# Two attention loops of a fused decoder kernel: row maxima ahead of the weight residues, and the second block's key and value panel between its two query panels

## Time and profile before

| | |
|---|---|
| median of three runs | 876.21 us (875.73 to 877.57) |
| profiled execution | 874.22 us, of which the span of the core is 872.4 us |
| TensorE (PE) busy | 815.5 us, 93% of the span |
| VectorE (DVE) busy | 549.2 us, 63% |
| ScalarE (ACT) busy | 420.5 us, 48% |
| GpSimd (POOL) busy | 115.0 us, 13% |
| mean granted TensorE clock | 0.978 of full speed |
| HBM | 119.48 MB read, 138 GB/s over the span |

### The profile page before, as it was taken

How to read it: one execution, slowest core, us unless ns; L and a number is a source line. 1 busy time by engine, 2 the same in 40 slices (tenths; PEclk the granted TensorE clock), 3 DMA queues, 4 the chain that set the end, 5 groups by cost and what they waited for, 6 DMA issues and landing times.

```text
span 872.4 us, 13760 instructions
## 1 busy us (share of the span) xinstructions
PE 815.5 (93%) x5402; PEld 721.7 (83%) x5402; DVE 549.2 (63%) x930; ACT 420.5 (48%) x820; POOL 115.0 (13%) x114
## 2 busy tenths in 40 slices
PE   5989898998969899999999999998999999999996
PEld 4768786876868677899988988888997788999995
DVE  5898666746895745444834757776674746555555
ACT  5434726744554634446536435554444435444443
POOL 1335004521441302000000000011000000000000
PEclk9999988999989999999999999998999999999999
DMA  9646222023543133463432544333454546655541
GB/s 311 198 154 205 85 72 74 1 72 120 181 131 107 54 109 108 153 200 131 145 121 73 162 129 145 97 98 119 160 181 145 193 145 217 195 192 193 184 155 48
DMA packets 93504, 121.42 MB, mean 139 GB/s; under 512 B 8760, under 2 KB 69616, under 8 KB 93440
## 3 DMA queue, kind: packets, MB, share of 16 engines
q1 hardware_dynamic: 92432, 117.80, 42.0%
q0 software_dynamic: 432, 1.57, 0.5%
q10 hardware_dynamic: 576, 1.17, 0.4%
HBM read 119.48 MB, written 1.05 MB: 138 GB/s over the span
## 4 chain that ended last, share of the span: by engine, by line
PE 75%; DVE 13%; ACT 4%; issue 3%; POOL 1%; POOLq 0%; DVEq 0%; ACTq 0%
PE bank L407 20%; PE bank L409 19%; PE bank L408 19%; DVE w_lo L1407 3%; PE bank L584 2%; PE bank L537 1%; PE bank L551 1%; ACT w_hi L1026 1%; PE bank L531 1%; ACT tmp L1124 1%; PE bank L892 1%; PE bank L414 1%; PE bank L413 1%; DVE small L1496 1%; DVE xres L1578 1%
## 5 line engine op out<-in xcount | busy, mean ns | idle before, releaser
L1407 DVE TENSOR_TENSOR w_lo<-raw,w_hi 128x1024 fp32r<-128x1024 f32 x216 | 267.0, 1242 | 154.7 <-ACT w_hi L1026 152.5
L1026 ACT CAST w_hi<-raw 128x1024 fp32r<-128x1024 f32 (+1 forms) x217 | 226.1, 1045 | 203.4 <-PE bank L409 181.6
L407 PE MATMUL bank<-h_hi,w_hi 128*128 128x256 f32 (+1 forms) x800 | 231.3, 289 | 2.6 <-DVE ar L1484 1.8
L408 PE MATMUL bank<-h_lo,w_hi 128*128 128x256 f32 (+1 forms) x800 | 228.1, 285 | 0.0
L409 PE MATMUL bank<-h_hi,w_lo 128*128 128x256 f32 (+1 forms) x800 | 227.4, 284 | 0.0
L407 PEld LDWEIGHTS bank<-h_hi,w_hi 128*128 128x128 f32 x800 | 152.5, 191 | 7.9 <-issue 3.4
L408 PEld LDWEIGHTS bank<-h_lo,w_hi 128*128 128x128 f32 x800 | 152.7, 191 | 0.3
L409 PEld LDWEIGHTS bank<-h_hi,w_lo 128*128 128x128 f32 x800 | 152.9, 191 | 0.0
L407 PE MATMUL bank<-w_hi,h_hi 128*128 128x512 f32 (+1 forms) x288 | 114.7, 398 | 11.5 <-DVE w_lo L1407 6.3
L409 PE MATMUL bank<-w_hi,h_lo 128*128 128x512 f32 (+1 forms) x288 | 112.6, 391 | 0.0
L408 PE MATMUL bank<-w_lo,h_hi 128*128 128x512 f32 (+1 forms) x288 | 112.1, 389 | 0.0
(11 more groups left out here) (309 smaller groups left out, 1245.1 us busy)
## 6 DMA issues: line engine op xcount, KB each, us to landing
raw<-in_w_in SPq DMA_DIRECT2D x24, 1024.0 KB, 5.2
raw<-in_a_w_in SPq DMA_DIRECT2D x14, 1024.0 KB, 5.2
raw<-in_w_ffn_gate SPq DMA_DIRECT2D x11, 1024.0 KB, 5.4
raw<-in_w_ffn_up SPq DMA_DIRECT2D x11, 1024.0 KB, 5.3
raw<-in_w_ffn_down SPq DMA_DIRECT2D x11, 1024.0 KB, 4.9
raw<-in_b_w_in SPq DMA_DIRECT2D x9, 1024.0 KB, 5.3
raw<-in_w_gate SPq DMA_DIRECT2D x8, 1024.0 KB, 5.3
raw<-in_a_w_out SPq DMA_DIRECT2D x4, 1024.0 KB, 5.1
```

The lines of the kernel that those rows point to most:

```text
L407: mm(o, lh, rh, start=start, stop=False)
L408: mm(o, lh, rl, start=False, stop=False)
L1026: nc.scalar.copy(split(w_hi, s), rawsub(s)[0]).then_inc(S["hi_ready"], 1)
L1407: V.tensor_tensor(split(w_lo, s), rawsub(s)[0], split(w_hi, s).bitcast(F), ALU.subtract).then_inc(S["lo_ready"], 1)
```

## The change

1. In both loops VectorE takes maxima and factors first; z gates and the rest follow, and the residues of the weights come last in a step, those that ScalarE has rounded a step earlier. ScalarE's roundings also move to the end of its step. In block 0 the residues of the four sub-chunks that the loop itself splits are spread to steps 10, 13 and 16 (`z_done`).
2. Block 0's compressed softmax is cut into four pieces that VectorE does in steps 0 to 3 of the loop; the transposes go to step 5 and bank 5, and quad 0's compressed values follow `pv(5)` instead of going ahead of `pv(0)`.
3. From job 4 (block 0) or 6 (block 1) on, scores rotate over banks 0 to 3, once the z tiles have left banks 0 and 1. `scores(j)` then waits for the exponentials of job j - 4.
4. In block 1 the key and value panel comes between the query panels (the order of the chunks in memory traffic follows), heads 0 to 7 are transposed ahead of the last quarter of the second query panel, keys after z tile 0, and heads 8 to 15 after z tile 1.
5. The transposes of the meta tokens go behind `scores(0)`, and the rest of their work on VectorE to the step after the last job's maxima.

```diff
-    tm("b_q", b, 512)
     add("b_kv", ...)
+    tm("b_q2", b, 512)
...
         def z_done(phase, j):
-            return 5 + min(j, 3) if phase == 0 else 3 + min(j, 5)
+            return 5 + min(max(j - 7, 0) // 3, 3) if phase == 0 else 3 + min(max(j, 0), 5)
+
+        def score_bank(phase, j):
+            return ps[2 + j % 2 if j < J4[phase] else (j - J4[phase]) % 4]     # J4 = (4, 6)
...
# TensorE, scores(j)
-                    if j >= 2:
-                        pe.wait_ge(S["p_exp"], j0 + j - 1)
+                    r = j - J4[phase]
+                    if r in (0, 1):
+                        pe.wait_ge(S["z_free"], 8 * phase + 7 + r)
+                    elif j >= 2:
+                        pe.wait_ge(S["p_exp"], j0 + j - 1 if r < 0 else j0 + j - 3)
...
# TensorE, block 1 ahead of its loop
             first_panel(1, first["b_q"], (0, 1))
-            tm_panel(first["b_q"] + 4, hx(h_hi), hx(h_lo), (2, 3))
+            tm_panel(first["b_kv"], hx(h_hi), hx(h_lo), (4, 5), width=256, rows=4)
+            tm_panel(first["b_q2"], hx(h_hi), hx(h_lo), (2, 3), last_q=3)
+            for tt in range(2):
+                pe.wait_ge(S["rp_out"], 9 + tt)
+                head_transposes(tt, 1, q_half(tt, 0))
+            tm_panel(first["b_q2"], hx(h_hi), hx(h_lo), (2, 3), first_q=3)
...
# VectorE, the loop
                 for j in range(n + LAG + 3):
-                    split_lo_to(z0 + z_done(phase, j) + RING)
-                    if phase and 1 <= j <= 5:
-                        z_gate(phase, 2 + j)
-                    if phase and j == 2:
-                        meta_tokens()
                     if j < n:
                         maxima(j)
                     if 1 <= j <= n:
                         factors(j - 1)
+                    if phase and 1 <= j <= 5:
+                        z_gate(phase, 2 + j)
+                    if phase == 0 and 1 <= j <= 2:
+                        z_gate(phase, 5 + j)
+                    if phase == 0 and j < 4:
+                        (compressed_sums, compressed_shift, compressed_factors, compressed_weights)[j]()
+                    if phase and j == 1:
+                        meta_tokens()
+                    if phase and j == n:
+                        meta_halves()
+                    if phase == 0 and j == 5:
+                        dve.wait_ge(S["cm_pt"], 1)
+                        V.tensor_copy(pcT, ps[5][:, :]).then_inc(S["cm_ptsb"], 1)
...
+                    split_lo_to(z0 + z_done(phase, j - 1) + RING)
...
# VectorE, block 1 ahead of its loop
+            base = first["b_q"] + 4
             for i in range(2):
+                split_lo_to(base + RING - 1 + i)
+                rope_item(10 + i, 11 + i, i, 8, 4, i, q8(i, 0), 8 + i)
+            for i in range(2):
+                split_lo_to(base + 2 + RING - 1 + i)
+                rope_item(12 + i, 13 + i, 4 + i, 2, 5, i, kd[2][:, i, 0:2], 10 + i)
...
+            for i in range(2):
+                q_lo(i, 12, 8 + i, i, 0)
+            split_lo_to(base + 5 + RING)
...
+            for i in range(2):
+                split_lo_to(base + RING - 1 + i)          # base = first["b_z"]
+                rope_item(14 + i, 15 + i, 2 + i, 8, 4, i, q8(i, 1), 12 + i)
+            z_gate(1, 0)
+            for i in range(2):
+                key_lo(2 + i, 10 + i, 0, i, 2)
+            split_lo_to(base + 1 + RING)
+            z_gate(1, 1)
+            for i in range(2):
+                q_lo(4 + i, 12, 12 + i, i, 1)
```

More of the change, by code:

```diff
@@ L427, in tm_half, with tm_panel @@
                 return last
-            def tm_panel(name_s, xh_, xl_, banks, width=512, rows=2):
-                for q in range(KT // rows):
+            def tm_panel(name_s, xh_, xl_, banks, width=512, rows=2, first_q=0, last_q=None):
+                for q in range(first_q, KT // rows if last_q is None else last_q):
                     s = name_s + q
@@ L506, in q_tiles, with q_half @@
                 return [[qr[:, tt, P * k:P * k + P] for k in range(4 * half, 4 * half + 4)] for half in range(2)]
+            def q_half(tt, half):
+                return [[qr[:, tt, P * k:P * k + P] for k in range(4 * half, 4 * half + 4)]]
             def k_tiles(i, groups):
@@ L563, in compressed_values @@
                         half = f // 4
-                        mm(ps[6 + quad % 2][:, T * (f % 2):T * (f % 2) + T], vblk[half][:, P * (f % 4):P * (f % 4) + P], pw[:, :, half, :],
-                           start=f % 2 == 0, stop=True, skip_group_check=f % 2 == 1)
+                        last = mm(ps[6 + quad % 2][:, T * (f % 2):T * (f % 2) + T], vblk[half][:, P * (f % 4):P * (f % 4) + P], pw[:, :, half, :],
+                           start=quad > 0 and f % 2 == 0, stop=True, skip_group_check=quad == 0 or f % 2 == 1)
+                    return last
                 def pv(j):
@@ L573, in pv @@
                         pe.wait_ge(S["og_ready"], 4 * phase + quad - 1)
-                    if phase == 0 and j % JQ[phase] == 0:
+                    if phase == 0 and quad and j % JQ[phase] == 0:
                         compressed_values(quad)
```

154 lines of the change are left out of this document (82 added, 72 removed).

## The result

| | before | after |
|---|---|---|
| median | 876.88 us (875.73 to 877.57, 4 runs) | 863.78 us (862.09 to 864.82, 4 runs) |
| ratio | | 0.985, interval 0.983 to 0.987 |
| profiled execution, span | 874.22, 872.4 us | 864.82, 863.0 us |
| mean clock of its TensorE | 0.978 | 0.982 |

The change gains 13.1 us by these medians; forecast were 7.3. The same kernel measured again (run after_again) gave 863.78 us against 875.14 of before (ratio 0.9861, 0.9842 to 0.9881), so 11 to 13 us is the gain. The direction was right and the size too small.

A forecast was written before the change was run, and what follows sets the result against it. TensorE was taken as nearly full (815.5 of 872.4 us), with VectorE or a ring of waits bounding around block 1's start. -3.7 - 4.4 + 0.8 = -7.3 us gave 866.9, plus 2.0 for the median 868.9 us; range 866 to 872.

The forecast's parts named there:

- term 1: Start of block 0's loop: job 8 starts 4.7 us earlier, 1.0 of it only put off, so 3.7 us gained.
- term 2: Block 1 ahead of its loop: the new panel order lets the loop begin 1.1 us earlier.
- term 3: Block 1's loop: exponentials released first bring the last pv 4.4 us earlier, with term 2 in it.
- the allowance for the clock: Loss of 0.8 us allowed for half clock behind TensorE's new waits in both blocks; ends 0 and 3.5.
- Cost 0, at most 1 us: Block 0's loop: residues spread to steps 10, 13 and 16 fit, leaving VectorE at 78%.
- the ring: Block 1's loop: from step 6 on VectorE's cycle of waits was to be the bound, taking back some gain.
- 4.7 us a step before: Block 1's loop: each of the old first steps was a ring of 4.7 us, against 4 us after.
- The replay: The new instruction lists of the changed stretches worked through with the old trace's durations, all at 2.4 GHz.
- Rival 1: No POOL and VectorE contention, clock stays up, block 1's meta work hides: 11.2 us less, 865.0 us; chance 0.14.

The follow-up runs named there:

- u_zdone: The changed kernel with the residues of block 0's loop's last four weight sub-chunks back in steps 1 to 3 instead of 10, 13 and 16: 866.4 us.
- zsteps: The changed kernel with block 0's three weight residues on VectorE in steps 9, 12 and 15 instead of 11, 14 and 17: 863.9 us.
- u_banks: The changed kernel with only the banks put back, scores in banks 2 and 3 alone: 867.0 us.
- meta_late: The changed kernel with the four meta token operations (meta_halves) behind block 1's loop instead of ahead of the last copy: 863.5 us.
- u_loop1: The changed kernel with only the order inside block 1's loop put back (weight rounding, residue and z gate ahead of the maxima): 866.9 us.
- fill: The changed kernel with unneeded matmuls in three TensorE waits (block 0's key transposes, block 1's z tile 0 and last transposes): 863.6 us.
- before_fill: The kernel before with unneeded matmuls in four TensorE waits, at block 0's loop start and ahead of block 1's loop: 872.9 us.
- best: The changed kernel with meta_halves behind the loop, residues of z tiles 0 and 1 ahead of the first query residues, and fills in four places: 856.75 us.
- best2: The kernel of best with block 0's loop residues in steps 9, 12 and 15: 858.4 us.

## Why the prediction fell short

**What bounds, and where.** Right: the gain is in the three stretches named, and behind them 0.35 us. Right as well that TensorE's waits and its clock are all there is to gain. Of the 4.3 us between the forecast 7.3 and the 11.6 of the stretches, 0.7 are in term 1, 0.2 in term 2, 2.6 in term 3, and 0.8 are the allowance for the clock. By the trace of after_again they are -0.1, -0.3, 2.7 and 0.8. Term 3 is the miss in both.

**Term 1, 3.7 forecast, 4.4 measured (3.6 in after_again).** The start gained more: job 8 is 20.83 us behind scores(0), forecast 22.6 and before 27.32. TensorE's wait at the compressed transposes was 1.48 and not 2.3 us, with 0.54 for POOL ahead of it, and scores(1) came 5.03 us behind scores(0) for 5.81, since z tile 6 ran at half for a shorter time; in after_again that step takes 5.90, and job 8 comes at 21.67. So 0.8 us of the difference is luck with the clock. "Cost 0, at most 1 us" for the spread residues failed: 1.2 us, two times 0.6, as u_zdone and zsteps show. VectorE takes them in steps 11, 14 and 17, each of which has a copy too; the two late places follow 11 and 17, which have the residues of a result besides. Behind them the next maxima and factors are late, and POOL with them (the wait of 0.37 us at 156.50; scores(14) to scores(15) take 2.52 us for 1.93). A busy share of 78% did not say that there was room in each step. The change of banks was to gain nothing in this full part; in the new order it gains 0.8 us (u_banks), at these same two places. In the old order, of which the forecast spoke, it wasn't tested.

**Term 2, 1.1 forecast, 1.3 measured (0.8 in after_again).** VectorE was idle for 2.11 us ahead of the residues of heads 0 to 7 (2.3 forecast), and TensorE waited 2.88 us at z tile 0 (2.7) and 2.61 at the last transposes (2.9); only the first of the two waits there was 0.17 for 2.1.

**Term 3, 3.3 more forecast, 5.9 measured: the step that failed.** It has the sentence "From step 6 on VectorE's ring is the bound". From scores(0) the forecast has scores(5) at 21.2 us, (8) at 27.6, (11) at 36.6 and the last product at 45.8; measured were 20.56, 26.79, 34.33 and 43.22 (after_again: 20.48, 26.72, 34.26 and 43.15). Most of the miss is between jobs 8 and 11: 9.0 us forecast, 7.54 measured. From job 6 to job 8 the distances are 1.98 and 1.93 us, TensorE's own work without a wait, and from job 8 to job 11 it waits only 0.72 us for POOL and 0.38 for VectorE's copy. The steps ahead of job 5 add 0.6 us to the miss, jobs 5 to 8 0.2, and the end 0.3. VectorE and POOL do hold each other up, with the durations forecast (a residue of 1.97, a multiplication of 1.94 us). The wait of 0.72 us stands behind that multiplication; it is what the contention costs here, and 1.0 was taken for it. So the ring was there, but nearly hidden behind TensorE's work. meta_halves were right: 1.1 us at the last copy (meta_late). "4.7 us a step before" was an average over unlike steps: 5.17 (half clock), 3.55, 3.95, 4.66, 6.57. u_loop1 shows that the old order costs nothing up to scores(4) and 4.2 us in all behind it. Before, scores(8) come 35.10 us behind scores(0): the forecast had gained 7.5 us there and gave 4.2 back by the end of the loop, measured are 8.3 and 2.4. Scores(8) in the trace of before:

```profile
294.97 0.50 PE L531 MATMUL bank<-msk,crr 128*128 128x512 f32 x1
```

**The clock, +0.8 forecast.** The replay ran at 2.4 GHz, so its terms already held what the old half-clock stretches cost, without naming it; the 0.8 us were for new ones behind the new waits. Those cost nothing: none behind the compressed transposes, one at z tile 0 that VectorE hides (fill), and in block 1's loop the clock is 1.00 for 0.93. In after_again one in front of that loop costs 0.5 us. Rival 1 (865.0 us) was nearest in time, in part by luck; of its three reasons one held (the clock stays up in the loops) and two failed (POOL and VectorE do hold each other up, and the meta work does not hide).

**From profile to median.** I added 2.0 us for the median of before, which is right. For the changed kernel it was the other way round: its profiled execution (864.82 us) is 1.0 above its median. The four medians of before beside the experiments (875.1 to 875.7) lie 1.2 to 1.7 below that of the result; so much of the 13.1 us may be scatter.

## What to carry to other kernels

Count TensorE's busy time of a stretch at the clock that the rows show, not as work: a wait in front of a stretch in which TensorE is full can cost its own length and then again at half clock (5.86 us for 4.32 in the first step of block 1's loop), while at z tile 0, where VectorE was the bound, half clock cost nothing. Filling a wait with unneeded matmuls and reading the length of the stretch behind it tells the two apart, and pays where TensorE comes last behind it. When work moves into a step of a full loop, look at what else the same engine has in that very step; the busy share of the stretch hides it.

## What the runs showed of the hardware

Most stretches at half clock begin near the end of a wait of TensorE of 2 us or more (94.3, 241.0 us in after; 134.3, 250.3, 260.6 and 291.3 in before), a few behind short waits and small matmuls (117.2 in before, behind 32 of 128x32). But they don't follow each such wait, and not always for as long. Behind the same wait of 2.7 us at the same instruction the clock was 1.00 in the traces of before and of after_again and 0.50 in that of after, which is the same kernel as after_again; TensorE is full in all three and does 26 matmuls in 6 us at full clock and 14 at half. Before, after_again and after:

```profile
57.31:63.31 6.00, 6.00 (x26) 4.94 (x27) 5.76 (x11) 1.20 (x2) 0.00 (x0) 1.00 0.70 207
```

```profile
57.42:63.48 6.06, 6.06 (x26) 4.97 (x27) 5.82 (x11) 1.25 (x2) 0.00 (x0) 1.00 0.71 205
```

```profile
57.44:63.50 6.06, 6.06 (x14) 4.81 (x15) 5.82 (x11) 0.51 (x1) 0.00 (x0) 0.50 0.70 205
```

Much of the difference of about 4 us between executions of one kernel goes with this: the changed kernel's times go from 860.5 us at a mean clock of 0.986 to 864.8 at 0.982. The Trainium skill, "TensorE: Matmul & The Clock Gate", Part 1, says that the number of matmuls at the low clock at a kernel's start differs between runs of the same kernel. The rows of after_again and after agree, for a wait in its middle. In the traces of fill, before_fill, best and best2 the clock was at half behind none of the filled waits; without a fill it was at half near the wait of 3.4 us at block 0's key transposes in every trace, and near that of 2.9 us at z tile 0 in all but u_banks.
